# Zeroing a stage's semaphores by ranges of neighbouring numbers, in a two-layer streaming encoder

## The chip, the core and the metric

The kernel runs on one core of a Trainium2 chip. The metric is the device time of one execution in microseconds (us), the median of several executions.

## What is computed

One inference step of an encoder with two layers, for 1,024 new frames of one stream (the prompt) and the next 32 frames of a running stream with 1,024 frames behind it (the sample). All data is float32. Each layer is, cut to what matters:

```python
h = rmsnorm(x)                                   # x: 1056 tokens x 1024
fox, swa, mla inputs = split(h @ w_in)           # 1024 x 2214
y_fox = attention(6 heads, causal, with forget gates)
y_swa = attention(6 heads, window of 128, sink, ALiBi)
y_mla = attention(4 heads, keys and values from a latent of 128)
x += concat(rms(y_fox), rms(y_swa), rms(y_mla)) @ w_out
a, b = split(rmsnorm(x) @ w_ffn_up)              # 1024 x 5632
x += (gelu(causal_conv3(a)) * b) @ w_ffn_down    # 2816 x 1024
```

The outputs are x and the new keys, values, gates, latents and convolution states of both streams.

## The kernel before, in words

The tokens are kept transposed: 128 partitions of features, eight chunks of features, and 1,056 token columns that are worked on in three thirds of 352. Float32 operands are split in a high and a low part, and each product is three matmuls on TensorE (PE): high by high, high by low, low by high.

The program is a sequence of **stages**. Each stage is one `nc.Block()`, with a body of instructions for each of the five engines: TensorE (PE), VectorE (DVE), ScalarE (ACT), GpSimd (POOL) and SyncE (SP, which issues the DMAs). Inside a stage the engines run freely and are ordered by semaphores. A block ends with a barrier: every engine drains and reports, and no engine starts the next block before all have reported. The stages, in order: `first_layer_in` (the first layer's input projection); then for each of the two layers `fox_rows`, `attend_prompt` for fox, `attend_prompt` for swa, `latents_and_samples` (sample attention and mla projections), `attend_prompt` for mla, `attend_latent_sample`, and `layer_out` (w_out, the feed-forward part, and in the first layer also the second layer's input projection).

A stage counts its steps upward on semaphores from zero, so its semaphores must be zero again before they are used anew. There are two sorts:

- Semaphores **of one stage**: `own_semaphores` (L2800) takes them on entry, yields them to the stage, and on exit calls `restart` (L2789) and gives them back. It takes 23 for `first_layer_in` (L2851), 20 for each `attend_prompt` (L1054), 19 for `latents_and_samples` (L1665), and 15 for `attend_latent_sample` (L1953). `fox_rows` and `layer_out` take none.
- Semaphores **of a layer**: `program` (L2811) takes them once and collects those that both layers use in a list of 100. `mixers` (L2860) calls `restart` on that list once in each layer, at L2894, straight behind the `restart` that ends `latents_and_samples` and ahead of the mla attention.

`restart` is a block of its own, in which only POOL has work: one `sem_clear` for each semaphore (L2796). The four other engines have empty bodies, go to the barrier at the block's end, and wait there. So there are 13 such blocks: one of 23; in each layer three of 20 (fox, swa, mla), one of 19, one of 100 and one of 15. Together that is 23 + 2 x 194 = 411 semaphores.

In the trace, `sem_clear` is the instruction EVENT_SEMAPHORE_RANGE_CLEAR on POOL's queue, with a first and a last number; the kernel before gives it a single number each time. The barrier that ends a block of `restart` carries the line L2791 (the `with nc.Block()` of `restart`), on all five engines.

**Numbers.** The allocator hands out free numbers from the front of a list that begins at 99 and ends at 255. The five semaphores of the output come first (99 to 103), then 2 of the layer's list (104, 105), then 10 that are not in it (106 to 115), then its 98 others (116 to 213). The stages take what is left. A number that is given back goes to the end of the list, and a stage gives its numbers back in the reverse order of taking.

Of the kernel before, what the change touches and what calls it, by code (L numbers as in the profile page):

```python
# [2785 lines left out]
                    pin.pool(pool, 1)  # L2786


def restart(nc, sems):  # L2789

    with nc.Block() as block:  # L2791

        @block.gpsimd
        def _(pool):
            for x in sems:
                pool.sem_clear(x)  # L2796


@contextmanager
def own_semaphores(nc, name, singles, several=()):  # L2800

    with ExitStack() as s:
        one = lambda n: s.enter_context(nc.semaphore(f"{name}_{n}"))
        sem = {n: one(n) for n in singles.split()}
        for n, m in several:
            sem[n] = [one(f"{n}{i}") for i in range(m)]
        yield sem
        restart(nc, [x for v in sem.values() for x in (v if isinstance(v, list) else [v])])
# [51 lines left out]
def mixers(nc, k, lay, places, proj, prep, used):  # L2860
# [25 lines left out]
    with ExitStack() as f:  # L2886
        km = rt("km", [P, 2 * QT + 1, MLAH, MQK], where=f)
        vm = rt("vm", [P, 2 * QT + 1, MLAH, HD], where=f)
        qm = rt("qm", [P, TT, MLAH, MQK], where=f)
        mixed.roots = rt("yrs", [P, mixed.GROUPS, TOK], where=f)  # L2890
        mixed.key_roots = rt("ykr", [P, QT, MLAH], where=f)
        mixed.keys = (km[:, QT:2 * QT], mixed.key_roots)
        latents_and_samples(nc, k, lay, places, proj, qm, km, vm, mixed, yT, prep.fs, caches)
        restart(nc, used)  # L2894
        left.close()
        with ExitStack() as f2:
            keep(f2, "y_early", mixed.EARLY * places.CHUNK)
            attend_prompt(nc, k, "mla", MLAH, MQK, lambda h: qm[:, :, h, :], lambda h: km[:, :, h, :],
                          lambda h, t: vm[:, t, h, :], lambda h: h, yT, 6, beside=mixed, gain=k.mgain[0:MQK, 0:1])
        tiles = [(P if j < QT else DEC, lambda u, j=j: km[0:P if j < QT else DEC, QT + j, u, :],  # L2900
                  lambda p, j=j: vm[0:P if j < QT else DEC, QT + j, 2 * p:2 * p + 2, :].rearrange("p h d -> p (h d)"))
                 for j in range(TT)]
        keep(f, "y_hi_kept", DC * places.CHUNK)
        attend_latent_sample(nc, k, lambda h: qm[0:DEC, QT, h, :], tiles, yT, 6, pout)
# [39 lines left out]
```

How the kernel before makes its waits and increments, by code:

```python
    def wait(self, n):  # L78
        self.eng.wait_ge(self.sem, self.base + n)
# [122 lines left out]
    def scale(self, dve):  # L202
        row = self.k.row
        dve.wait_ge(self.rows_in, 16 * len(self.free))
        for at, n, d in ((R_FQ, HD, HD), (R_SQ, HD, HD), (R_MQ, MQK, MQK)):
            last = dve.tensor_scalar(row[:, at:at + n], row[:, at:at + n], float(d) ** -0.5, None, ALU.mult)
        last.then_inc(self.scaled, 1)
        dve.wait_ge(self.scaled, 1)
        mq = row[:, R_MQ:R_MQ + MQK]
        dve.tensor_tensor(mq, mq, row[:, R_MK:R_MK + MQK], ALU.mult).then_inc(self.scaled, 1)
# [37 lines left out]
    def store(self, sp):  # L248
        for t in range(TT):
            n = self.rows(t)
            sp.wait_ge(self.staged, t + 1)
            sp.dma_start(self.k.x_dram[:, :, t * P:t * P + n], self.stage[t][:, :, :])\
                .then_inc(self.tile_moved[t], 16)
# [5 lines left out]
    def turn_vectors(self, pe, l):  # L259
        ident = self.k.const[:, C_ID:C_ID + P]
        pe.wait_ge(self.const_in, 16)
        pe.wait_ge(self.feats_in[l], 16 * 7)
        if l:
            pe.wait_ge(self.vec_ready, l)
        pe.transpose(self.bank[:, 7, 2 * l * P:(2 * l + 1) * P], self.vst[:, 2 * l, :], ident)
        pe.transpose(self.bank[:, 7, (2 * l + 1) * P:(2 * l + 1) * P + self.rest], self.vst[0:self.rest, 2 * l + 1, :],
                     ident[0:self.rest, 0:self.rest]).then_inc(self.vec_turned, 1)
# [23 lines left out]
    def scalar(self, act, t):  # L291
        n, k = self.rows(t), self.k
        act.wait_ge(self.gained, t + 1)
        at = slice(t * P, t * P + n)
```

## Time and profile before

| | |
|---|---|
| median of 3 executions | 3150.83 us (3137.93 to 3152.77) |
| the profiled execution | 3160.54 us |
| span of its trace, from the first to the last instruction | 3158.7 us |
| mean granted TensorE clock | 0.953 of full speed |

How to read it: "busy" counts the instructions that do work on an engine; semaphore, barrier and branch instructions are not counted as busy, and carry a "q" behind the engine's name (POOLq is POOL's own queue of such instructions). An entry such as "PE psXmla L1149 <- PEq L2791" says that TensorE's next work was held up by an instruction of line L2791 on its own queue. PEclk is the clock that was granted to TensorE, in tenths of its full speed.

### The profile page before, as it was taken

What the parts mean: (1) busy time and instruction counts of PE and PEld (TensorE: products, weight loads), DVE (VectorE), ACT (ScalarE), POOL (GpSimd) and SP (SyncE); (2) the same over time, 40 slices, a digit from 0 to 9 for tenths busy, and PEclk for the clock granted to TensorE, in tenths of its full rate; (3) what the DMA queues carried; (4) which work ended last, traced back from release to release, by engine and by line L of the source; (5) the groups of instructions that cost most, each with busy time, mean ns of one, the idle gap of its engine ahead of it and who ended that gap; (6) DMA issues with size and microseconds to landing.
All of it is one profiled execution on the core that took longest, in us unless ns stands there. A gap on an engine that the chain in (4) does not pass through costs nothing. (4 is left out here: it accounts for less than half of the span.)

```text
span 3158.7 us, 52087 instructions
## 1 busy us (share of the span) xinstructions
PE 2943.3 (93%) x20666; PEld 2767.2 (88%) x20666; DVE 1572.9 (50%) x2761; ACT 994.8 (31%) x2263; POOL 950.1 (30%) x676
## 2 busy tenths in 40 slices
PE   6997989689999999999999988978899999999998
PEld 6996765569999999999999977647799999999998
DVE  3337775654344444444452576757334444444443
ACT  4334664543311111111243355646332111111111
POOL 3112433224323222223241143514143222232320
PEclk9998988789999999999999988979899999999999
DMA  5120010013411111111221201000143111111111
GB/s 165 39 69 24 2 60 10 1 35 103 144 46 47 46 40 40 53 40 43 62 75 39 79 2 60 10 1 1 50 154 96 40 40 53 40 45 48 45 48 56
DMA packets 181286, 161.87 MB, mean 51 GB/s; under 512 B 17268, under 2 KB 168348, under 8 KB 180892
## 3 DMA queue, kind: packets, MB, share of 16 engines
q1 hardware_dynamic: 181148, 160.02, 16.2%
q8 instruction: 87, 1.43, 0.2%
q14 instruction: 51, 0.42, 0.0%
HBM read 129.97 MB, written 30.13 MB: 51 GB/s over the span
## 5 line engine op out<-in xcount | busy, mean ns | idle before, releaser
L2373 PE MATMUL bank_b<-x_hi,fwhi 128*128 128x352 f32 x2112 | 689.8, 327 | 5.7 <-POOL fwlo L2329 5.7
L2373 PE MATMUL bank_b<-x_hi,fwlo 128*128 128x352 f32 x2112 | 688.1, 326 | 0.0
L2373 PE MATMUL bank_b<-f_lo,fwhi 128*128 128x352 f32 x2112 | 686.4, 325 | 0.0
L2329 POOL TENSOR_TENSOR fwlo<-raw,fwhi 128x1024 fp32r<-128x1024 f32 x132 | 321.6, 2436 | 580.8 <-ACT fwhi L2454 568.8
L2373 PEld LDWEIGHTS bank_b<-x_hi,fwhi 128*128 128x128 f32 x2112 | 399.3, 189 | 6.9 <-POOL fwlo L2329 6.3
L2373 PEld LDWEIGHTS bank_b<-f_lo,fwhi 128*128 128x128 f32 x2112 | 401.5, 190 | 0.0
L2373 PEld LDWEIGHTS bank_b<-x_hi,fwlo 128*128 128x128 f32 x2112 | 398.1, 188 | 0.6
L2562 DVE TENSOR_TENSOR fx<-fx,bank_b 128x352 f32<-128x352 f32 x528 | 275.7, 522 | 242.7 <-PE bank_b L2403 242.7
L2403 PE MATMUL bank_b<-fuhi,fwhi 128*128 128x352 f32 x1056 | 343.9, 326 | 4.5 <-DVE fulo L2556 4.5
L2403 PE MATMUL bank_b<-fulo,fwhi 128*128 128x352 f32 x1056 | 345.6, 327 | 0.0
L2403 PE MATMUL bank_b<-fuhi,fwlo 128*128 128x352 f32 x1056 | 345.0, 327 | 0.0
L2474 ACT ACTIVATE fuhi<-fcb 128x1024 fp32r<-128x1024 f32 x44 | 46.7, 1061 | 696.3 <-PE bank_b L2403 550.8
L2338 POOL TENSOR_TENSOR fcb<-fcb,rsb 128x1024 f32<-128x1024 f32 x44 | 96.8, 2200 | 510.8 <-ACT fcb L2468 510.8
L2403 PEld LDWEIGHTS bank_b<-fuhi,fwhi 128*128 128x128 f32 x1056 | 202.1, 191 | 5.6 <-issue 4.8
L2403 PEld LDWEIGHTS bank_b<-fulo,fwhi 128*128 128x128 f32 x1056 | 199.8, 189 | 0.0
L2403 PEld LDWEIGHTS bank_b<-fuhi,fwlo 128*128 128x128 f32 x1056 | 199.3, 189 | 0.0
L617 PE MATMUL bank_a<-whi,x_hi 128*128 128x246 f32 x576 | 163.9, 284 | 14.3 <-POOL x_lo L330 11.6
L555 POOL TENSOR_TENSOR wlo<-wraw,whi 128x1968 fp32r<-128x1968 f32 x18 | 82.5, 4582 | 278.6 <-ACT whi L564 278.6
L617 PE MATMUL bank_b<-whi,x_hi 128*128 128x246 f32 x576 | 161.7, 281 | 2.0 <-DVE x_lo L2629 1.7
L617 PE MATMUL bank_a<-wlo,x_hi 128*128 128x246 f32 x576 | 162.9, 283 | 0.0
L617 PE MATMUL bank_a<-whi,x_lo 128*128 128x246 f32 x576 | 162.9, 283 | 0.0
L617 PE MATMUL bank_b<-whi,x_lo 128*128 128x246 f32 x576 | 161.7, 281 | 0.0
(452 smaller groups left out, 6118.1 us busy)
## 6 DMA issues: line engine op xcount, KB each, us to landing
raw<-in_w_ffn_up SPq DMA_DIRECT2D x88, 512.0 KB, 3.8
raw<-in_w_ffn_down SPq DMA_DIRECT2D x44, 512.0 KB, 3.6
wraw<-in_w_in SPq DMA_DIRECT2D x18, 984.0 KB, 5.3
xs<-x_between SPq DMA_DIRECT2D x16, 528.0 KB, 3.9
x_between<-xs SPq DMA_DIRECT2D x16, 528.0 KB, 2.6
fx<-x_between SPq DMA_DIRECT2D x2, 4224.0 KB, 13.1
raw<-in_w_out SPq DMA_DIRECT2D x16, 512.0 KB, 5.3
x_between<-fx SPq DMA_DIRECT2D x3, 1408.0 KB, 5.7
```

The lines of the kernel that those rows point to most:

```text
L555: pool.tensor_tensor(self.wlo[b][:, :, :], self.raw[b][:, :, :], self.whi[b][:, :, :].bitcast(F32), ALU.subtract)\
L617: last = pe.matmul(bank[0:n, t % NB, 0:WN], a[:, c, at], w[b][:, c, :], start=(c == 0 and m == 0), stop=(c == DC - 1 and m == 2))
L2329: pool.tensor_tensor(self.wlo[:, r], self.raw[:, o % 2], self.whi[:, r].bitcast(F32), ALU.subtract)\
L2338: pool.tensor_tensor(v, v, self.rsb[:, 0:SEQ], ALU.mult)
L2373: last = pe.matmul(bank[:, first_bank + t, 0:TN], w[:, role, c, :], x[:, c, self.cols(t)], start=(c == 0 and m == 0), stop=(c == DC - 1 an ...
L2403: last = pe.matmul(bank[:, 6 + o % 2, 0:TN], w[:, D0 + e, m, :], x[:, e, self.cols(t)], start=(e == 0 and i == 0), stop=(e == 1 and i == 2))
L2474: act.activation(uhi[:, e, 0:SEQ], cb[:, e, 0:SEQ], ACT.Copy)
L2562: dve.tensor_tensor(x, x, bank[:, 6 + o % 2, 0:TN], ALU.add).then_inc(self.p_out[o % 2], 1)
```

## The change

`restart` no longer issues one clear for each semaphore. A new function sorts the numbers, joins neighbours to ranges, and issues one clear for each range. Nothing else of the program changes: the same numbers are zeroed, in the same 13 blocks, with the same barriers.

```diff
+def clear(pool, sems):
+
+    first = last = None
+    for n in sorted(x.num for x in sems) + [None]:
+        if first is not None and n != last + 1:
+            pool.sem_clear(range(first, last + 1))
+            first = None
+        if first is None:
+            first = n
+        last = n
+
+
 def restart(nc, sems):
 
     with nc.Block() as block:
 
         @block.gpsimd
         def _(pool):
-            for x in sems:
-                pool.sem_clear(x)
+            clear(pool, sems)
```

## Rows read from the trace of the kernel before

**Rows 1.** The page's head, busy times, and the granted clock in 40 slices.

```profile
span 3158.7 us, 52087 instructions
...
PE 2943.3 (93%) x20666; PEld 2767.2 (88%) x20666; DVE 1572.9 (50%) x2761; ACT 994.8 (31%) x2263; POOL 950.1 (30%) x676
...
PEclk9998988789999999999999988979899999999999
```

**Rows 2.** The line L2796 in the whole span: operation, count, duration ns min/median/max.

```profile
L2796 POOLq EVENT_SEMAPHORE_RANGE_CLEAR  x411: 44/44/48, 258.3 to 2257.1; - x137
```

**Rows 3.** L2796 in seven stretches: count, duration, first and last start.

```profile
L2796 POOLq EVENT_SEMAPHORE_RANGE_CLEAR  x23: 44/44/48, 258.3 to 259.8; - x23
...
L2796 POOLq EVENT_SEMAPHORE_RANGE_CLEAR  x20: 44/44/44, 400.9 to 402.3; - x20
...
L2796 POOLq EVENT_SEMAPHORE_RANGE_CLEAR  x19: 44/44/44, 572.9 to 574.2; - x19
...
L2796 POOLq EVENT_SEMAPHORE_RANGE_CLEAR  x100: 44/44/44, 574.5 to 581.8; - x100
...
L2796 POOLq EVENT_SEMAPHORE_RANGE_CLEAR  x15: 44/44/44, 703.1 to 704.1; - x15
...
L2796 POOLq EVENT_SEMAPHORE_RANGE_CLEAR  x19: 44/44/44, 2126.1 to 2127.7; - x19
...
L2796 POOLq EVENT_SEMAPHORE_RANGE_CLEAR  x100: 44/44/44, 2128.0 to 2135.0; - x100
```

**Rows 4.** Line L2791 (end of a block), stretch 258 to 261.

```profile
L2791 POOLq EVENT_SEMAPHORE  x2: 17/17/17, 260.0 to 260.1; - x2
L2791 SPq DRAIN  x1: 7/7/7, 258.3 to 258.3; - x1
...
L2791 PEldq DRAIN  x1: 13/13/13, 258.4 to 258.4; - x1
L2791 POOLq DRAIN  x1: 46/46/46, 259.9 to 259.9; - x1
...
L2791 PEldq EVENT_SEMAPHORE  x1: 51/51/51, 260.1 to 260.1; - x1
```

**Rows 5.** Busy time of each engine over two boundaries, and two stretches behind the first.

```profile
core 0: us, PE busy (x) PEld busy (x) DVE busy (x) ACT busy (x) POOL busy (x), PEclk, DMA share, GB/s
...
572.90:582.20 9.30, 0.00 (x0) 0.00 (x1) 0.00 (x0) 0.00 (x0) 0.00 (x0) 0.50 0.00 1
...
2126.00:2135.30 9.30, 0.00 (x0) 0.00 (x0) 0.00 (x0) 0.00 (x0) 0.00 (x0) 0.50 0.01 2
...
582.00:595.00 13.00, 9.42 (x41) 8.50 (x42) 4.43 (x11) 4.67 (x16) 0.61 (x1) 0.51 0.00 0
595.00:666.00 71.00, 64.69 (x558) 54.53 (x555) 64.20 (x124) 50.68 (x134) 35.38 (x33) 1.00 0.01 1
```

**Rows 6.** Waits of the stretch 574 to 600.

```profile
ACT qThimla L1224 <- PE psXmla L1150: 18.8, 6, 12.3
...
PE psXmla L1149 <- PEq L2791: 15.2, 1, 15.2
```

**Rows 7.** Instructions in order of time, first ones after four boundaries.

```profile
402.60 1.80 POOL L1125 MEMSET kThiswa<- 32x2048 f32 x1 [31.86 <-POOLq L2791]
...
479.04 0.77 DVE L1856 COPY km<-proj 128x1024 f32<-128x1024 f32 x1 [3.79 <-PEq L2791]
...
582.23 0.42 PE L1149 MATMUL psXmla<-const,qm 128*96 128x128 f32 x1 [15.20 <-PEq L2791]
...
676.52 1.01 SPq L2101 DMA_DIRECT2D raw<-in_w_out  x2
```

**Rows 8.** In order of time: the last store, and L1017 of the first layer.

```profile
257.56 0.35 SPq L801 DMA_DIRECT2D out_swa_v_p<-proj  x1
...
265.43 1.21 DVE L1017 SCALAR_TENSOR_TENSOR frowlo<-fpsF,frowhi 6x1024 fp32r<-6x1024 f32 x1 [2.89 <-ACT frowhi L1007]
```

**Rows 9.** The chain of work that ended last: its first piece.

```profile
2257.49 0.04 issue
```


## The prediction

> **What bounds the kernel now.** The page's head comes first: TensorE is busy 93% of a span of 3158.7 us, and the granted clock is near full in most slices [rows 1]. The kernel is bound by TensorE wherever it runs, so only time in which TensorE stands still can be saved by an edit on POOL. POOL is busy 30%, and its clears are not in that number, since semaphore instructions don't count as busy. So the page can't show the cost of the clears, and I go to the line itself.
>
> The line of the clear runs 411 times at 44 ns each [rows 2]. The duration is not the price, though: its stretches give the distance from start to start. 23 clears take 1.5 us from the first start to the last, 20 take 1.4, 15 take 1.0, 19 take 1.3, the second hundred 7.0 [rows 3]. Divided by one less than the count that is 0.068, 0.074, 0.071, 0.072 and 0.071 us; these readings are rounded to 0.1 us, and the longest one is the most exact: **0.071 us per clear**. Two stretches are longer by 0.3 us than that: the first hundred (7.3), and the nineteen of the second layer (1.6 against 1.3) [rows 3]. In each of them POOL stopped once.
>
> Next is whether anyone waits. In the first of the 13 blocks SP and PE drain at 258.3 and 258.4, POOL drains only at 259.9, behind its last clear, and all are released at 260.1 [rows 4]. So POOL alone ends the block. Over the 9.3 us from the first of the nineteen to the mla stage, in either layer, every engine is at 0.00 us busy and the DMA share is at most 0.01 [rows 5]. The last view is what comes right behind: POOL, DVE, PE and SP start at once, and the rows of the first three name the barrier as what they waited for [rows 7]; the mla stage's first matmul waited 15.2 us by its row and went straight on [rows 6, 7]. The chain of waits says little here: its first piece starts at 2257.49, just behind the last clear at 2257.1, and it was not followed through a barrier [rows 2, 9].
>
> **The change, part by part.** Every block of clears keeps its barrier. What changes is how many clears stand ahead of it. From the order in which the numbers are handed out and given back, the ranges are:
>
> - the 23 of the first stage: 214 to 236, 1 range;
> - first layer: fox 1 (236 to 255), swa 1 (216 to 235), the nineteen 3, the hundred 2 (104 to 105, 116 to 213), mla 2, the fifteen 2;
> - second layer, where the free list has been turned over several times: fox 4, swa 3, the nineteen 4, the hundred 2, mla 3, the fifteen 5.
>
> That is 1 + 11 + 21 = 33 clears in place of 411, so 378 fall away. Of these, 196 are in the two blocks of a hundred.
>
> *Removed.* 378 x 0.071 = **26.8 us**, all in time in which the other engines stand at the barrier.
>
> *The two stops of 0.3 us* [rows 3]. They come with many clears in a row, as if POOL had run out of instructions. With 378 fewer instructions they may go (0.6 us saved) or fall elsewhere (0). I take half, 0.3 us.
>
> *The barrier's floor.* PE drains 0.1 us behind the first clear [rows 4]. With one or two clears POOL is no longer the last by much: at worst each of the 13 blocks loses 0.1 us, 1.3 us in all. Three blocks go down to one clear and four to two, the others keep more; I take 0.3 us.
>
> *A clear of a wide range.* No row shows one: all 411 name a single number. From below it costs what a clear of one costs, 44 ns, and 0.071 from start to start. From above, the nearest row is POOL's ordinary semaphore instruction, which takes 17 ns [rows 4]: if the other 27 ns of the clear are work per number, each further number of a range costs 27 ns, and 378 further numbers cost 10.2 us. Further still, each number could cost the whole 71 ns, and nothing is gained. I take the low end, since the opcode has a first and a last number and its shortest and middle durations are the same 44 ns [rows 2], as a fixed sequence would have it; the other value stays for the range.
>
> A rule of the Trainium skill speaks against the low end. The page "Runtime: NRT & Kernel Launch", under "The ~15µs preamble/postamble breakdown", gives about 1.5 us for the reset of 51 semaphores per engine behind a kernel, 29 ns for each. By it, as an estimate, 378 further numbers would cost 11.1 us and the gain would be 15.7. No row here shows that reset, so the trace neither agrees nor disagrees.
>
> *Moved.* Nothing on any queue changes order. Each stage starts earlier together with all its DMAs, so transfers issued in a stage keep their distance from its work. One thing does not move with the clears: a transfer issued ahead of a boundary and awaited behind it. The last store of the input projection is issued at 257.56, and the next stage's SP waits for it; but that stage's end is set by DVE's step that starts at 265.43, eight us behind the store and five behind the barrier [rows 4, 8], which is cover enough for 1.6 us. The first w_out loads are issued at the start of the stage that ends 27 us later [rows 3, 7].
>
> *Sum.* 26.8 + 0.3 - 0.3 = 26.8 us. Against the profiled execution's 3160.54 us (span 3158.7 and 1.8 around it) this gives 3133.7. That execution is 9.7 us above the median of the three, which itself has neighbours from 3137.93 to 3152.77; the same sum from the median of 3150.83 gives **3124.0 us**, and I put the forecast there.
>
> **The rivals.** (a) *A range costs 27 ns for each further number.* For it: the 44 ns against 17 ns of another semaphore instruction [rows 2, 4]. Against it: nothing but that the opcode is made for ranges. Gain 26.8 - 10.2 = 16.6 us, so 3134.2.
>
> (b) *The saved standstill comes back as slow clock.* Behind the hundred, TensorE runs at 0.51 of full clock for 13 us, with 9.42 us of it busy, then at 1.00 [rows 5]. If the moment at which the clock returns stays where it was while the work starts 7 to 8 us earlier, the earlier part runs at half speed and gives back up to half of what was saved. Over all boundaries that is at most 13.4 us, so 3137.4. Against it: the clock rose in the 595 us stretch after TensorE had been at work for some 13 us, so it should follow the work; and the start of a stage is a chain from PE to ACT to DVE, in which ACT waits for PE six times [rows 6], and ACT and DVE don't slow with TensorE's clock.
>
> (c) *No gain.* Either the numbers are hardly neighbours, so that the change doesn't do what it says, or each number in a range costs the full 71 ns. The hundred's 98 neighbours exclude the first. 3150.8.
>
> (d) *Slower.* The range clear is the mechanism here too: its place is the two blocks of a hundred, where the 98-wide range stands. If each further number costs more than 71 ns, all of the saving is lost; at 113 ns the 378 cost 42.7 us against 26.8, and the time is 3166.7. From 71 ns on, this decides. No row excludes it, but a clear of one number would then be by far the cheapest per number, at 44 ns in all.
>
> **How the numbers follow.** Forecast 0.62, (a) 0.23, (b) 0.07, (c) 0.05, (d) 0.03. A measurement of this kernel can tell about 0.5% from no change, 15.8 us, so the border is 3135.1. The forecast lies 11 us below it, against an unsure few us from the medians: all but 0.01 of it is faster. (a) lies just inside: 0.14 faster, 0.09 within. (b) spans 3124 to 3137: 0.02 faster, 0.05 within. (c) is within, (d) slower. Sum: faster 0.77, within 0.5% 0.20, slower 0.03. The range runs from 3114 (the forecast, with the two stops and 9 us for the spread of the runs shown) up to 3138, which takes in (a) and (b); it leaves out (c), (d) and the tails.
>
> **What would show it.** In the changed profile the clears should number 33, each at about 44 ns; a range of 98 at 2.7 us instead says (a), at 7 us (c), longer (d). The distance from POOL's release behind the nineteen to the mla stage's first matmul should fall from 9.3 us to about 1. TensorE's busy time should stay at 2943 us; if it rises by several us with the stretches of half clock behind the boundaries, (b) is right. The boundaries of 20 should each shrink by 1.1 to 1.3 us. The forecast is wrong if the wide clears are long, or if the stages behind the boundaries are longer than before by what the boundaries lost.

## The result, and the profile after the change

| | before | changed |
|---|---|---|
| median | 3151.20 us (3134.18 to 3166.57, 14 executions) | 3123.95 us (14 executions; 13 of them 3117.40 to 3138.95) |
| ratio | | 0.9937, 95% interval 0.9917 to 0.9957 |
| profiled execution | 3160.54 us | 3122.45 us |
| mean granted clock in it | 0.953 | 0.962 |

One execution of the changed kernel took 7153.13 us: it counts in that median and is left out of the range and the ratio, and the median of the other 13 is 3122.45 us. The ratio says 0.63% less (0.43 to 0.83), or 20 us of 3151; the two medians lie 27 us apart, the two profiled executions 38 us. Three figures for one edit: most of what follows is about why they differ.

The page of the changed kernel, its head, its busy times and the granted clock in 40 slices, beside [rows 1]:

```profile
span 3120.7 us, 51709 instructions
...
PE 2927.0 (94%) x20666; PEld 2756.3 (88%) x20666; DVE 1572.4 (50%) x2761; ACT 995.4 (32%) x2263; POOL 952.9 (31%) x676
...
PEclk8998999889999999999999989989899999999999
```

There are 378 instructions fewer (52087 - 51709), exactly the clears that went. But TensorE is busy for 16 us less as well, with the same 20666 matmuls, none of which the edit touches. What differs for them is the clock, 0.962 against 0.953.

Now the clears, on L2794 in the changed kernel: the whole span, then five stretches (count, duration min/median/max in ns, first and last start), beside [rows 2, 3]:

```profile
L2794 POOLq EVENT_SEMAPHORE_RANGE_CLEAR  x33: 44/46/565, 259.8 to 2216.5; - x33
...
L2794 POOLq EVENT_SEMAPHORE_RANGE_CLEAR  x1: 158/158/158, 259.8 to 259.8; - x1
...
L2794 POOLq EVENT_SEMAPHORE_RANGE_CLEAR  x1: 136/136/136, 400.9 to 400.9; - x1
...
L2794 POOLq EVENT_SEMAPHORE_RANGE_CLEAR  x3: 44/45/113, 560.2 to 560.4; - x3
...
L2794 POOLq EVENT_SEMAPHORE_RANGE_CLEAR  x2: 45/305/565, 560.8 to 560.8; - x2
...
L2794 POOLq EVENT_SEMAPHORE_RANGE_CLEAR  x2: 45/305/565, 2095.9 to 2096.0; - x2
```

33 clears, as many as the prediction counted. A range of 23 takes 158 ns, one of 20 takes 136, and the range of 98 takes 565 (the longer of the two in each of the last two stretches). The stretch that took from 574.5 to 581.8 now holds two clears, 0.07 us apart.

The barrier behind the first of these blocks (L2803, POOL's own queue and TensorE's loads), beside [rows 4]:

```profile
L2803 POOLq EVENT_SEMAPHORE  x2: 17/17/17, 260.1 to 260.2; - x2
...
L2803 PEldq DRAIN  x1: 13/13/13, 259.9 to 259.9; - x1
L2803 POOLq DRAIN  x1: 46/46/46, 260.0 to 260.0; - x1
...
L2803 PEldq EVENT_SEMAPHORE  x1: 51/51/51, 260.2 to 260.2; - x1
```

TensorE and POOL now drain within 0.1 us of each other, at 259.9 and 260.0, and all are released at 260.2, against 259.9 for POOL and 260.1 for all before, in a block whose first clear starts at 259.8 instead of 258.3. The block has shrunk from 1.8 us to 0.4.

The two boundaries with the hundred, and the 13 us behind the first (us, busy time of each engine, clock, DMA), beside [rows 5]:

```profile
core 0: us, PE busy (x) PEld busy (x) DVE busy (x) ACT busy (x) POOL busy (x), PEclk, DMA share, GB/s
...
560.20:561.70 1.50, 0.00 (x0) 0.00 (x0) 0.00 (x0) 0.00 (x0) 0.00 (x0) 0.50 0.00 0
2095.20:2096.90 1.70, 0.02 (x1) 0.06 (x2) 0.00 (x0) 0.00 (x0) 0.00 (x0) 0.50 0.01 5
561.70:574.70 13.00, 9.60 (x43) 8.67 (x44) 4.55 (x12) 4.68 (x16) 0.61 (x1) 0.52 0.00 0
```

The 9.3 us are 1.5 and 1.7. Behind them, the mla stage starts as it did: its first matmul names the barrier, after an idle time of 7.4 us where it was 15.2 [rows 7], and the clock stands at 0.52 for 13 us, with 9.60 us of TensorE busy where it was 9.42.

```profile
561.75 0.42 PE L1149 MATMUL psXmla<-const,qm 128*96 128x128 f32 x1 [7.42 <-PEq L2803]
```

Summed over the eleven boundaries, from the start of the first clear to the end of the last, the clears take 29.9 us in the trace before and 4.4 us in the one of the changed kernel: **25.5 us less**. The span lost 38.0. The idle time of TensorE that ended at a barrier behind a block of clears fell by nearly the same, from 53.2 to 28.2 us over the eleven boundaries: 25.0 us. The half microsecond between the two is a stop of POOL that came up at a new place: behind the clears of 681 us POOL's drain starts at 681.6 and takes 174 ns, where the other engines had drained at 681.2. So about 12.5 us of the difference between the two traces lie elsewhere. One stage holds more than that, `latents_and_samples`. It stands here for both layers, before and after:

```profile
479.00:572.90 93.90, 80.50 (x290) 47.40 (x290) 56.88 (x125) 43.68 (x110) 31.29 (x51) 0.77 0.03 8
2032.00:2126.00 94.00, 80.63 (x290) 47.33 (x290) 56.69 (x125) 43.68 (x110) 31.23 (x51) 0.77 0.03 8
```

```profile
474.90:560.20 85.30, 70.16 (x290) 40.97 (x290) 56.87 (x125) 43.71 (x110) 31.27 (x51) 0.90 0.03 9
2010.20:2095.30 85.10, 69.93 (x290) 40.29 (x290) 56.86 (x125) 43.71 (x110) 31.36 (x51) 0.89 0.03 9
```

The instructions are the same (290 matmuls, and DVE, ACT and POOL are busy for the same time to within 0.2 us, whatever TensorE's clock). The stage took 94 us before and 85 after, twice 9 us, and what differs with it is the clock, 0.77 against 0.90 and 0.89, and with the clock TensorE's own busy time, matmuls (80 against 70 us) and weight loads. Others gave some of it back: from the last clear behind `attend_latent_sample` of the first layer to the first one behind the fox attention of the second, a stretch that is mostly `layer_out`, it was 1249.6 us before and 1253.2 after. The question for the runs was therefore how much of the 38 us is the edit, and whether the clock's part belongs to it.

### The profile page after: what moved, and what is told of

Read it like the earlier page. It is cut to its first block and busy times, and to the rows that moved or that the text cites. A ratio compares the mean times of both kernels' runs of the same rounds, so it can differ in the third digit from the quotient of the medians.

```text
span 3120.7 us, 51709 instructions
## 1 busy us (share of the span) xinstructions
PE 2927.0 (94%) x20666; PEld 2756.3 (88%) x20666; DVE 1572.4 (50%) x2761; ACT 995.4 (32%) x2263; POOL 952.9 (31%) x676
## 5 line engine op out<-in xcount | busy, mean ns | idle before, releaser
L617 PE MATMUL bank_a<-whi,x_hi 128*128 128x246 f32 x576 | 163.7, 284 | 14.9 <-POOL x_lo L330 12.1
```

The source lines that it names most:

```text
L617: last = pe.matmul(bank[0:n, t % NB, 0:WN], a[:, c, at], w[b][:, c, :], start=(c == 0 and m == 0), stop=(c == DC - 1 and m == 2))
```

## The experiments

Theory A: each boundary costs its own length, and the clock is a lottery that has nothing to do with the change. Theory B: the length of the boundaries also decides where the clock falls behind them, so that part of the saving is given back for good. Each set ran beside the kernel before on the same chip. The results together, as ratios to the executions of before of the same set:

| kernel | executions, us (median) | ratio, 95% interval | clears in its trace |
|---|---|---|---|
| changed, again (e1_after) | 12: 3115 to 3139 (3126.4) | 0.9933 (0.9912 to 0.9954) | 4.4 us |
| changed, again (e2_after) | 9: 3118 to 3139 (3130.3) | 0.9931 (0.9903 to 0.9959) | 4.4 us |
| ranges in the hundred alone | 9: 3121 to 3136 (3130.1) | 0.9945 (0.9923 to 0.9967) | 16.8 us |
| ranges in the small blocks alone | 12: 3131 to 3149 (3139.4) | 0.9977 (0.9958 to 0.9996) | 17.9 us |
| before, every clear twice | 6: 3174 to 3182 (3181.7) | 1.0105 (1.0076 to 1.0134) | 60.3 us |
| ranges, padded to the old length | 12: 3138 to 3171 (3151.0) | 1.0014 (0.9990 to 1.0038) | 32.2 us |
| changed, one boundary 0.85 us longer | 6: 3120 to 3130 (3126.2) | 0.9919 (0.9894 to 0.9943) | 6.4 us |
| changed, 12 transposes more | 6: 3120 to 3127 (3125.4) | 0.9914 (0.9883 to 0.9945) | 4.4 us |
| no blocks of clears (e2_behind) | 6: 3100 to 3111 (3109.6) | 0.9857 (0.9825 to 0.9889) | none at a boundary |
| no blocks of clears (e3_behind) | 6: 3101 to 3111 (3107.8) | 0.9862 (0.9836 to 0.9887) | none at a boundary |
| both of these | 6: 3097 to 3107 (3103.7) | 0.9855 (0.9830 to 0.9880) | none at a boundary |

**The changed kernel again.** No edit.

> The changed kernel again, beside the one before on the same chip. Theory A (the saving is the clears' own time, 25.5 us less at the eleven boundaries as the two traces show, and the rest of the 38 us between the two profiled executions is TensorE's clock, which falls differently in each execution): 25 us less than before in the mean, single executions some 16 us apart from each other in two groups. Theory B (the clock gives part of it back for good, since every boundary now falls at another moment): 15 to 20 us less, and at equal mean clock still less than 25.

> The changed kernel a third time, now beside the kernels of this set. Theory A: 25 us less than before (ratio 0.992); its interval so far reached from 14 to 28 us, and its executions again lie in groups some 9 and 18 us apart, by whether the sample stage of a layer (latents_and_samples) takes 85 or 94 us. Theory B: 15 to 20 us less (0.9945).

The three sets of the changed kernel agree: 0.9937, 0.9933, 0.9931. All executions taken together, 34 of it have a mean of 3127.1 us and 71 of before have one of 3148.2, a difference of 21.1 us, 95% interval 17.9 to 24.3. That is 4 us less than the 25.0 to 25.5 that left the boundaries, and these lie outside the interval, though inside that of each set alone. The executions spread over 24 us here and over 32 before, without the two groups that Theory A named.

The comparison at equal clock, which the first of these texts names, does not settle it. Lines through the executions give 17 us less at a mean clock of 0.960. But some 17 us of the standstill that went had lain at half clock (0.50 over the 9.3 us), and taking it out raises the mean clock by itself: an estimate from these numbers is 0.002, and the clock rose from 0.9587 to 0.9605. What the edit may have moved beyond that is smaller than these executions resolve.

One execution of the second of these sets shows where the spread comes from, since it has the stage `latents_and_samples` in both lengths. First the whole stage in either layer, then, for each, 4 us around a wait of TensorE and 19 us behind it, and last the two matmuls that end that wait:

```profile
472.50:557.70 85.20, 70.21 (x290) 40.90 (x290) 56.96 (x125) 43.70 (x110) 31.27 (x51) 0.90 0.03 9
2007.90:2103.50 95.60, 81.58 (x290) 47.32 (x290) 56.92 (x125) 43.71 (x110) 31.20 (x51) 0.77 0.03 8
...
517.00:521.00 4.00, 1.96 (x10) 0.97 (x8) 3.83 (x12) 3.04 (x8) 0.00 (x0) 1.00 0.00 0
521.00:540.00 19.00, 16.75 (x90) 12.83 (x90) 15.04 (x37) 10.55 (x31) 1.20 (x5) 0.85 0.01 1
2056.00:2060.00 4.00, 1.41 (x7) 0.66 (x6) 3.79 (x10) 3.08 (x8) 0.00 (x0) 1.00 0.00 0
2060.00:2079.00 19.00, 18.37 (x65) 12.73 (x63) 10.92 (x27) 9.52 (x26) 0.00 (x0) 0.50 0.00 1
...
521.66 0.30 PE L1598 MATMUL mpsT<-const,spr 128*64 128x128 f32 x1 [2.59 <-ACT proj L1793]
...
2058.80 0.30 PE L1598 MATMUL mpsT<-const,spr 128*64 128x128 f32 x1 [2.59 <-ACT proj L1793]
```

The stage takes 85 us in the first layer and 96 in the second. In both layers TensorE stands still for the same 2.59 us, until ACT has copied out the PSUM bank that the next transposes write (L1793). The first of the two 4 us windows holds only a part of this wait, hence its 1.96 us busy against 1.41. In the 19 us of the next window the clock is at 0.85 of full speed in the first layer and at 0.50, the lower level of 1.2 GHz throughout, in the second. Over the stage that makes 0.90 and 0.77. In the twelve traces without the transposes that a later run adds to that stage, its length was 84 to 88 us fifteen times and 94 to 96 us nine times. So an execution has none, one or two long stages, at some 9 us each. The instructions and the wait are the same in both forms and the clock is not, so the clock makes the length; what makes the clock fall in one and not in the other is not shown.

**Half of the change.** In one kernel the ranges are used in the blocks of a hundred alone (the condition below), in the other in all but these.

```diff
-            clear(pool, sems)
+            if len(sems) == 100:
+                clear(pool, sems)
+            else:
+                for x in sems:
+                    pool.sem_clear(x)
```

> Ranges only in the two blocks of a hundred, single clears in the other eleven. 196 clears fewer at 0.071 us, less two wide ones at 0.565 us: 13.9 + 0.6 for a stop of POOL - 1.0 = 13 us less than before by theory A. By theory B 8 to 10. The 98-wide clear should last 0.565 us again, and the rest of the boundaries stand as before (1.39 us for a block of 20).

> Ranges only in the eleven small blocks, single clears in the two of a hundred. 182 clears fewer at 0.071 us, less about 1 us for the longer ones: 12 us less than before by theory A; the two halves add up to the whole change. By theory B the halves need not add up: 8 to 10 each, or one of them near 0.

The hundreds' ranges gained 17.3 us (interval 10.4 to 24.2) where their boundaries lost 13.1; the small ones gained 7.2 (1.3 to 13.2) where theirs lost 12.1. Theory A's 13 and 12 lie inside both intervals. Theory B's 8 to 10 lies inside the second and just below the first, but of the two halves it asked only that they need not add up. The halves sum to 24.5 us, which is near the 25.5 and not clear of the 20 to 22 of the whole. These two runs say that both kinds of block count, and don't tell A from B.

**Every clear twice.**

```diff
-            for x in sems:
+            for x in sems + sems:
                 pool.sem_clear(x)
```

> The kernel before with every clear issued twice, 822 in all. By theory A each clear costs 0.071 us of the program: 411 x 0.071 = 29.2 us more than before. If the clears were partly hidden, or if the clock made up for them, it would be under 20.

The clears in its trace take 30.3 us more, and the executions 33 us more (24 to 42). So the clears are not hidden behind other work. In this trace one effect of the clock shows beside it: `attend_latent_sample`, first in the kernel with double clears, then in the changed one.

```profile
684.50:713.80 29.30, 22.15 (x109) 16.29 (x109) 7.26 (x16) 6.74 (x12) 4.71 (x2) 0.56 0.13 37
```

```profile
654.40:681.10 26.70, 19.55 (x109) 14.51 (x109) 7.27 (x16) 6.75 (x12) 4.70 (x2) 0.66 0.15 40
```

The same instructions take 29.3 us with the clock at 0.56 behind the longer standstill, and 26.7 at 0.66 behind the short one; so it is in the second layer (29.0 against 26.3). In the kernel before, behind 1.4 us of clears, it took 26.9 in both. A boundary of twice the old length costs more than its length here.

**The price of a wide clear.** A block ahead of everything else:

```diff
+            for w in (1, 2, 4, 8, 12, 16, 24, 32, 48, 64, 98):
+                for _ in range(3):
+                    pool.sem_clear(range(116, 116 + w))
```

> The changed kernel with a block of clears ahead of everything: ranges of 1, 2, 4, 8, 12, 16, 24, 32, 48, 64 and 98 numbers, each three times. The theory that a range costs 27 ns and 5.5 ns for each number, with a floor of 44 ns: 44, 44, 49, 71, 93, 115, 159, 203, 291, 379 and 566 ns. A cost in steps (of 8 or 16 numbers, say) would show as equal durations for neighbouring widths.

The stretches of that line in order of time. The median is that of the width which fills most of the stretch: 1, 2, 4, 12, 16, 24, 32, 48 and 98 numbers.

```profile
L2868 POOLq EVENT_SEMAPHORE_RANGE_CLEAR  x4: 44/44/48, 0.7 to 0.9; - x4
...
L2868 POOLq EVENT_SEMAPHORE_RANGE_CLEAR  x3: 45/45/45, 0.9 to 1.1; - x3
...
L2868 POOLq EVENT_SEMAPHORE_RANGE_CLEAR  x2: 47/47/47, 1.2 to 1.3; - x2
...
L2868 POOLq EVENT_SEMAPHORE_RANGE_CLEAR  x3: 90/92/92, 1.7 to 1.9; - x3
...
L2868 POOLq EVENT_SEMAPHORE_RANGE_CLEAR  x4: 112/112/155, 2.0 to 2.4; - x4
...
L2868 POOLq EVENT_SEMAPHORE_RANGE_CLEAR  x4: 155/155/198, 2.4 to 3.0; - x4
...
L2868 POOLq EVENT_SEMAPHORE_RANGE_CLEAR  x4: 198/198/285, 3.0 to 3.7; - x4
...
L2868 POOLq EVENT_SEMAPHORE_RANGE_CLEAR  x4: 285/285/372, 3.7 to 4.6; - x4
...
L2868 POOLq EVENT_SEMAPHORE_RANGE_CLEAR  x3: 565/565/565, 5.8 to 7.0; - x3
```

It is a straight line with a floor: 44 to 47 ns up to four numbers, then 92, 112, 155, 198, 285 and 565 ns. From 24 to 48 numbers it rises by 130 ns, 5.4 for each; from 48 to 98 by 280, 5.6 for each. The widths of 8 and 64, which no stretch above shows by itself, took 68 to 70 and 372 ns. There are no steps. This kernel ran once, and its time is not compared.

**Ranges, padded to the old length.**

```diff
             clear(pool, sems)
+            for x in sems[len(sems) // 12:]:
+                pool.sem_clear(x)
```

> Ranges as in the changed kernel, and behind them single clears of the same numbers, until each of the 13 blocks is about as long as before (some 1 us longer over all). If standstill at the boundaries is all that the change acts through, this is the kernel before: ratio 1.000, with executions from 3134 to 3166. If it were the number of numbers zeroed, or ranges as such, it would lie nearer to the changed kernel.

1.0014 (0.9990 to 1.0038), with executions from 3138 to 3171. Its clears take 2.3 us more than those of the kernel before, and not 1. With boundaries of about the old length the kernel is the old one, to within 3 us less and 12 more: the ranges as such gain nothing, and the change acts through the time at the boundaries.

**One boundary 0.85 us longer.** Twelve single clears more in the block between the swa attention and `latents_and_samples`, in each layer.

```diff
+            for _ in range(fill):
+                pool.sem_clear(sems[0])
...
-    with own_semaphores(nc, "att", "...", [("row", 2)]) as sem, \
+    with own_semaphores(nc, "att", "...", [("row", 2)], 12 * swa) as sem, \
```

> The changed kernel with 12 single clears more (0.85 us) in one block of each layer, that between the swa attention and latents_and_samples. Theory A (each boundary costs its own length): 1.7 us slower than the changed kernel, 23 us faster than before. Theory B (a boundary's length also sets where in the clock's rhythm the next stage starts): the sample stage starts 0.85 us later against the moments at which the clock changes, where its length was 94 us in the traces so far; more than 3 us slower than the changed kernel, up to 15, with fewer executions below 3122.

Theory B failed in this form: the kernel is not slower than the changed one in its other sets (there was none in this set). Its ratio is 0.9919, 26 us less than before (18 to 33), where A gave 23. Its first sample stage lasted 88.1 us and its second 94.4, so the long form still occurs. The run can't tell a loss of 1.7 us from none.

**Twelve transposes more.** They stand in `latents_and_samples` of each layer, ahead of TensorE's wait for the normalised probabilities and behind its wait for the bank; later transposes write over their results.

```diff
         swa = part == 3
+        if swa and g == 0:
+            for _ in range(12):
+                pe.transpose(psT[0:R, 3, 0:R], ident, ident)
         pe.wait_ge(self.normed[swa], g + 1)
```

> The changed kernel, with 12 transposes more on TensorE in latents_and_samples of each layer, into a bank that is free, where TensorE waits 2.6 us for the normalised probabilities; their results are overwritten. If the two lengths of that stage (85 and 94 us) come from TensorE's clock falling behind this wait and staying at half speed for some 30 us: the stage takes 86 us in both layers of every trace, and the executions lie closer together and 5 to 9 us lower in the mean than the changed kernel's. If the clock is not the cause, nothing changes, or it is 2 us slower for the extra work.

Both stages of its trace, and the added transposes of the first:

```profile
473.10:563.10 90.00, 73.00 (x302) 42.03 (x302) 56.77 (x125) 43.65 (x110) 31.16 (x51) 0.89 0.03 9
2009.60:2094.50 84.90, 69.59 (x302) 40.06 (x301) 56.59 (x125) 43.71 (x110) 31.00 (x51) 0.91 0.03 9
...
524.07 1.53 PE L1597 MATMUL mpsT<-const 128*128 128x128 f32 x12 [2.59 <-ACT proj L1796]
```

The edit did not do what it was meant to. The transposes write the bank that ACT is still copying out, and this was the wait of 2.59 us, not the one for the probabilities: DVE had normalised these by 519.8. So TensorE stands still as long as before, in both layers, and the transposes follow as 1.5 us more work behind the wait.

Neither is long, though the first is 90 us and not 86. The six executions lie within 7 us (3120 to 3127), while those of the changed kernel in the same set reach from 3118 to 3139; the ratio is 0.9914 against 0.9931, with intervals that overlap. So the executions did lie closer together and the time did not grow with the work, but not because TensorE was kept at work in the wait. Whether the wait has a part in the two lengths was not tested, and the mean gain was not resolved.

**No blocks of clears.** The numbers of a stage are held for one stage longer and zeroed, by ranges, at the start of POOL's work in the next one, behind the barrier that the stage has anyway. The list of a hundred is zeroed at the start of the mla attention. The 13 blocks and their barriers go. Cut to its core:

```diff
+def clear_old(pool):
+
+    clear(pool, Behind.old)
+    Behind.held, Behind.old = Behind.old, []
...
             @block.gpsimd
             def _(pool):
+                clear_old(pool)
                 smp.zero(pool)
...
     yield sem
-    restart(nc, [x for v in sem.values() for x in (v if isinstance(v, list) else [v])])
+    release_held(nc, Behind.kept)
+    Behind.old = [x for v in sem.values() for x in (v if isinstance(v, list) else [v])]
```

> No blocks of clears at all: a stage's semaphores are zeroed, by ranges, at the start of POOL's work in the stage behind it, and their numbers are given back only at that stage's end. The 13 blocks and their barriers are gone. Theory A (what is paid for is standstill at the boundary): the 4.4 us that the clears and the two inner barriers still take go, and some 0.3 us for each of the other eleven barriers: 7 to 8 us less than the changed kernel, 32 less than the one before (0.990). If POOL's late start held up a stage, the gain over the changed kernel would be near 0.

> The kernel without blocks of clears again: it was 20 us faster than the changed one where 7 to 8 were expected, in six executions that all lay within 11 us. If that was luck in where the clock fell, these executions spread over 16 us as the changed kernel's do, with a mean 8 us below it. If its stages start at moments that keep the sample stage short, they stay between 3100 and 3111.

It is the fastest single edit by far: 0.9857 and 0.9862, some 44 us less than before and 20 less than the changed kernel, in both sets, with all twelve executions between 3100 and 3111. Its first mla matmul, in order of time:

```profile
557.57 0.42 PE L1153 MATMUL psXmla<-const,qm 128*96 128x128 f32 x1 [5.99 <-PEq L1701]
```

TensorE's idle time ahead of it is 6.0 us where the changed kernel had 7.4, so a boundary with a hundred is shorter by 1.4 us. Over all eleven boundaries this idle time falls from 28.2 to 20.3 us, 7.9 less, which is what was expected (7 to 8). The other 12 us are not explained by boundaries. They go with the clock: these twelve executions have a mean granted clock of 0.967, and the 34 of the changed kernel one of 0.961, among which 0.01 more of clock goes with 26 us less. In both of its traces the sample stages are short (85.2 and 86.6 us, 85.3 and 86.4), and no execution lies where one with a long stage would. The range that was put down for the repeat held. That the stages start at moments which keep the sample stage short is the reason it gave, and it was not tested.

**Both together.**

> Both together: clears behind the stage's start, and the 12 transposes in TensorE's wait. If the transposes only help where the sample stage would be long, and it is short without blocks of clears anyway: within 3 us of e3_behind. If both stages of the kernel without blocks are still long now and then: some us faster and closer together.

0.9855 (0.9830 to 0.9880), executions from 3097 to 3107, sample stages of 84.9 and 84.8 us. It is 4 us by the median from the kernel without blocks, near the 3 that were expected where the stage is short anyway. Here too the transposes run behind the wait of 2.59 us and not in it. It is the lowest median of all (3103.7 against 3107.8), by less than these six executions resolve.

## Why the prediction was right, point by point

- **The count.** 33 clears in 13 blocks: exact, and so are the 378 instructions that went.
- **The price of a clear, 0.071 us from start to start, all on the path.** Right. Doubling them cost 33 us for 30.3 us of clears, and padding them back gave the old time.
- **The wide clear, taken at its low end.** This term was mis-sized, by little: 5.4 to 5.6 ns for each number beyond the floor, neither 0 nor 27. Over the 33 clears of the changed trace, durations beyond 44 ns add up to 1.9 us, 0.5 of it in each clear of 98. So 26.8 becomes 24.9. For the same reason the 9.3 us became 1.5 and 1.7 and not about 1.
- **The two stops of POOL.** Both are gone from their places, 0.6 us, and 24.9 + 0.6 = 25.5 us is what the clears lost. But a stop of some 0.45 us came up behind the clears of 681 us, so that TensorE's standstill lost 25.0. The prediction had left open whether they go or fall elsewhere; the truth lies between.
- **The barrier's floor, 0.3 us.** Not seen: with one clear the release came 0.2 us after the start of POOL's drain, as before.
- **Rival (a), 27 ns per number, and the rule of the Trainium skill.** The page "Runtime: NRT & Kernel Launch" of the Trainium skill gives about 1.5 us for the reset of 51 semaphores per engine behind a kernel, under "The ~15µs preamble/postamble breakdown"; the 29 ns for each are an estimate from it. A range clear takes 565 ns for 98, 5.8 ns each with everything in. The measurement decides: that estimate is not the price of this instruction. No run shows the reset that the page speaks of.
- **Rival (b), the saved standstill coming back as slow clock.** Its mechanism was looked for in the wrong place. Behind the hundred the clock followed the work: 0.52 for 13 us after as before. But some 4 us of the 25.0 to 25.5 did not arrive in the mean of the executions (21.1, interval 17.9 to 24.3), and it is the clock that makes `latents_and_samples` 9 us longer in one execution than in another, and the stretch with `layer_out` 3 us. Whether it takes these 4 us for good, and by what, stays open: the run that was to show it (0.85 us more at one boundary) did not.
- **TensorE's busy time should stay at 2943 us.** Wrong: it fell to 2927, because the two traces caught the sample stages in their long and their short form. The sign that was named for rival (b) can't be read from one pair of traces.
- **The number.** 3124.0 forecast, 3123.95 measured. That close a hit is luck: the measured median counts the execution of 7153 us (3122.45 without it), and the median of 3150.83 from which the forecast starts was that of three executions. By the mean of all executions the gain is 21 us and not 27, and the other two medians of the changed kernel were 3126.4 and 3130.3. The gain lies beyond the border of 0.5% in its middle (0.63%), though the interval of the first comparison reaches to 0.9957, over that border.

## What to carry to other kernels

Semaphore housekeeping that runs alone between two barriers is paid in full, at its start-to-start distance and not its duration, and the page's busy shares don't show it: look at the lines of the boundary itself. Zeroing by ranges takes most of it; putting the zeroing behind the next stage's start, where POOL has nothing urgent, also takes the block and its barrier, and here was worth as much again, of which 7.9 us are standstill that went and the rest goes with a higher clock that nothing here explains. Where the executions of a kernel differ by more than the edit, compare the same stretches of several traces first: the difference of two profiled executions (38 us) was half as large again as the edit's own 25.5.

## What the runs showed of the hardware that was not expected

- EVENT_SEMAPHORE_RANGE_CLEAR on POOL: 44 to 47 ns for up to four numbers, then about 26 ns and 5.4 to 5.6 for each number, 565 ns for 98. Single clears in a row stand 71 ns apart, so one clear of 98 costs what eight single ones do.
- A stage took 85 or 95 us with the same instructions and the same wait of 2.59 us in its middle. In the execution that has both, the clock was at half speed for the whole of 19 us behind the wait in one layer, and for a part of them in the other.
- Behind 2.8 us of clears `attend_latent_sample` took 29.3 us, behind 0.2 us of them 26.7: the clock's mean over the stage was 0.56 and 0.66.
